# New TensorE durations in the planner of a two-block kernel: delta rounds and column norms

## The chip, the cores and the metric

The kernel runs on one core of one Trainium2 chip. The metric is the device time of one execution, in microseconds (us), from start to end on that core.

## The reference, cut to what matters

Two transformer-like blocks run one after the other on 1024 tokens of width 1024. The change touches the planning of two parts of the first block.

```python
# first block, delta branch: projection, depthwise convolution of 5 taps, silu, l2norm of q and k
qkv = silu(conv(concat([dq, dk, dv])))
dq, dk = dq * rsqrt(sum(dq * dq) + EPS), dk * rsqrt(sum(dk * dk) + EPS)   # per token and head of 128
# gated delta recursion, 4 heads of 128, two directions, chunks
def step(S, inp):
    v_new = u_c - w_c @ S
    o = (q_c * exp(g_c)) @ S + a_c @ v_new
    S = S * exp(g_last) + (k_c * exp(g_last - g_c)).T @ v_new
    return S, o
```

The same block has a neighbourhood attention branch; the second block has stick-breaking attention, chunked retention and three projections. The first block ends in an output projection whose input is the attention branch and the delta branch side by side, so the second block can't begin before the delta recursion is over.

## The kernel before, in words

**Layout.** All large projections are matmuls in three passes over split operands (`g` items: one of eight steps of one tile, lines 1781 to 1783 and 1787 to 1789). Weights come through a ring of raw buffers and are split into a high and a low part by ScalarE and VectorE (`w` items). The first block works through the blocks `dn0` to `dn3` (delta projections), `na0` to `na3` (attention), `dz` (gates), then has a stretch with no projection, in which the delta recursion is done, and then `wo0` and `wo1`, the output projection.

**The planner.** `schedule()` writes one list of items before anything is built. Class `Plan` keeps one clock for each engine, and streams (generators) that put items. `work(item)` gives an item's steps, each with an engine and a duration in ns. `put` moves each step to the later of the stream's time and its engine's clock, adds `HOP` (150 ns) after each step, and advances the engine's clock. `pump` lets every stream go on whose time is no later than TensorE's clock, in order of rank and time. Nothing of the durations is written into the kernel; what comes out is the order of the list. Every engine, and the DMA queues of SyncE and GpSimd, runs its part of the items strictly in the order of that list, with semaphore waits between engines. Which items exist, and what each does, doesn't depend on the durations. The order does, and with it the PSUM banks that `take` hands out to some of the items.

**The items that the change touches.**

- `cn` (h, c), eight of them, in the convolution's stream: 8 matmuls of 128x128 by one column, which sum the squares of the convolved q and k (line 1913), and a small evacuation on VectorE (line 2665).
- `r0` (h, s), the first third of round s of head h, for s from 1: 4 matmuls 128x128x128 (lines 1992 and 1995), then VectorE's residual (2725) and ScalarE's scaled copy of the query product beside it (2127 is the helper's line).
- `r1` (h, s): 2 matmuls (line 2011), then ScalarE's scaled copy and its plain copy of 128x256.
- `r2` (h, s): 2 matmuls for the state (line 2018, not in round 7) and 2 for the output (2023), then VectorE's update of the state (2735) and its add into the output (2742 and 2747).

**The items around them.** A round of a head is a chain: r0, r1, r2, and the next round's r0 waits for this round's state and output. Four heads, of 8 rounds each, run interleaved. A head may begin when its loads have landed (`dl`, `dv`, `dt` on SyncE's queue) and its levels `e0` to `e3` (a triangular inverse, lines 1950 to 1976) are done. After round 7 of a head come `f1` (square on ScalarE, line 2380; sums and a refined rsqrt on VectorE with ScalarE between, 2751 to 2759) and `f2` (two products of 128x1024 on VectorE, 2767 and 2770), then two `st mxd` items (transposes, line 1747). The other half of the output projection's input comes through `ld mix` (SyncE's queue), `mz` (GpSimd, 2972) and `st mix` (transposes). `wo0` begins when these are there.

Of the kernel before, what the change touches and what calls it, by code (L numbers as in the profile page):

```python
# [19 lines left out]
class Plan:  # L20
# [6 lines left out]
    def __init__(self, work):  # L27
        self.items, self.known = [], {}
        self.clock = dict(pe=0.0, act=0.0, dve=0.0, pool=0.0, dma=0.0, bus=0.0)
        self.streams, self.now, self.work = [], None, work  # L30
# [263 lines left out]
def work(item):  # L294
# [3 lines left out]
    def act(n):  # L298
        return "act", 170 + 0.87 * n

    def dve(n):
        return "dve", 130 + 1.08 * n
# [16 lines left out]
    if kind == "d9":  # L319
        return [("pool", 2700)]  # L320
    if kind == "r0":
        return [("pe", 450), ("dve", 690), ("act", 640, "beside")] if a[1] else []
    if kind == "r2":
        return [("pe", 450), ("dve", 620), ("act", 400) if a[1] == 0 else ("dve", 430)]
    if kind in ("ns", "np", "no"):
        n = 12 * COLS[a[2] % 4][1]
        return {"ns": [("pe", 60 if a[1] else 2.2 * n), dve(n + 90), act(n + 340)], "np": [("pe", 340), act(384)],
# [8 lines left out]
    if kind == "rm":  # L336
# [34 lines left out]
        "pa": [("dma", 4000)],  # L371
        "cs": [("act", 3700)],
        "cq": [act(1024)],
        "cn": [("pe", 900), ("dve", 150)],
        "d3": [("act", 900), ("dve", 400), ("act", 300)],
        "d4": [dve(1024)],
        "dm": [("pool", 1300)],
# [7 lines left out]
        "e1": [("pe", 800), ("dve", 850), ("act", 400, "beside")],  # L385
        "e2": [("pe", 500), act(512)],
        "e3": [("pe", 500), dve(512)],
        "r1": [("pe", 230), ("act", 640), ("act", 390)],
        "fz": [("dma", 5000)],
        "f1": [act(1024), dve(1024), ("dve", 300), ("act", 400), ("dve", 200)],  # L390
        "f2": [dve(1024), dve(1024)],
# [19 lines left out]
def schedule():  # L411

    plan = Plan(work)
    put, has = plan.put, plan.has
    place = {}
# [2755 lines left out]
```

How the kernel before makes its waits and increments, by code:

```python
    def wait_ge(self, sem, value):  # L123
        if self.seen.get(id(sem), 0) < value:
            self.seen[id(sem)] = value
            self.eng.wait_ge(sem, value)
# [1371 lines left out]
        def released(w, before):  # L1498
            if before:
                for said in freed(before):
                    w.wait_ge(*said)
# [64 lines left out]
        @block.sync  # L1567
# [3 lines left out]
            def load(n):  # L1571
                if n >= n_w:
                    return
                if n >= NRAW:
                    w.wait_ge(*at["w", n - NRAW, "lo"])
                if 72 <= n < 76:
                    for h in range(4):
                        w.wait_ge(*at["e3", h, 1, "o"])
                c0 = 0
                for s in weights(n)[1]:
                    wd = s.shape[1] if len(s.shape) == 2 else s.shape[1] * s.shape[2]
                    d = RAW[:, n % NRAW, c0:c0 + wd]
                    if len(s.shape) == 3:
                        d = d.rearrange("p (s c) -> p s c", c=s.shape[2])
                    e.dma_start(d, s).then_inc(c_raw[n % NRAW], 16)
                    c0 += wd
# [19 lines left out]
                    for n in range(72, 76):  # L1606
                        load(n)
                elif kind == "nx":
                    p = a[0]
                    w.wait_ge(*at["nz", p, "z"])
                    e.dma_start(z_d[p].rearrange("(t p) k -> p t k", p=128), tokens(p % 2)[:, :, 384:512]).then_inc(c_nz[p % 2], 16)
                elif kind == "gw":
                    w.wait_ge(*at["gr", "out"])
                    e.dma_start(g_d, GTs).then_inc(c_g, 16)
```

## Time and profile before

| what | value |
|---|---|
| median of 3 runs | 2236.14 us (2234.33 to 2240.19) |
| the profiled execution's own time | 2240.78 us |
| its span, first to last instruction | 2238.9 us |
| mean granted TensorE clock | 0.981 of full |
| TensorE matmuls busy | 2155.8 us (96%) |
| VectorE, ScalarE, GpSimd busy | 1086.3, 943.1, 386.1 us |

The profile is one execution with the hardware profiler. A busy TensorE is not TensorE at its peak, since matmuls overlap. The granted clock is a share of full speed, where 1.00 is 2.4 GHz and 0.50 is 1.2 GHz. Where a line says `x4`, four instructions of that line are merged; each 128x128 fp32 matmul of the source is two matmul instructions in the trace, a transpose is one.

### The profile page before, as it was taken

To read this page: it belongs to the slowest core of one execution; us is meant where nothing else is said; L and a number is where in the kernel's file an instruction comes from. 1 tells how busy PE (TensorE), PEld (TensorE's weight loads), DVE (VectorE), ACT (ScalarE), POOL (GpSimd) and SP (SyncE) were. 2 spreads that over 40 slices of the span, in tenths; PEclk is the share of its full clock that TensorE was granted. 3 is DMA by queue.
4 is the path that set the end of the run, shared out by engine and by line. 5 is a ranking of instruction groups with operands and counts; after the bars stand their busy time and mean duration, and the time that the engine had idled before them with its cause. 6 is when DMAs were issued, how large, how long until landed. Compare 5 with 4: busy or idle time off the path is not lost.

```text
span 2238.9 us, 29041 instructions
## 1 busy us (share of the span) xinstructions
PE 2155.8 (96%) x11559; PEld 1775.5 (79%) x11559; DVE 1086.3 (49%) x2025; ACT 943.1 (42%) x1712; POOL 386.1 (17%) x594
## 2 busy tenths in 40 slices
PE   7999999997887999999999999999999999999998
PEld 5787777776886888887888788887888878888887
DVE  5776444431366334667456755546425242433441
ACT  4655454553463234655455645643132313232220
POOL 5011452563013010000000000005202020110011
PEclk9999999999797999999999999999999999999999
DMA  4455454433724221122111111012221212344222
GB/s 146 134 191 180 115 147 127 109 98 119 310 70 165 72 86 38 39 71 62 48 34 57 57 57 39 29 33 71 85 71 34 62 34 88 101 157 140 94 93 86
DMA packets 169672, 209.76 MB, mean 94 GB/s; under 512 B 36320, under 2 KB 122816, under 8 KB 168000
## 3 DMA queue, kind: packets, MB, share of 16 engines
q1 hardware_dynamic: 148848, 140.71, 20.3%
q0 software_dynamic: 20688, 67.19, 9.4%
q8 instruction: 91, 1.49, 0.3%
q14 instruction: 45, 0.37, 0.1%
HBM read 150.41 MB, written 53.77 MB: 91 GB/s over the span
## 4 chain that ended last, share of the span: by engine, by line
PE 90%; DVE 3%; ACT 2%; DMA 2%; issue 2%; POOL 1%; SPq 1%; DVEq 0%; POOLq 0%; ACTq 0%
PE PS L1787 14%; PE PS L1789 13%; PE PS L1788 13%; PE PS L1781 9%; PE PS L1783 9%; PE PS L1782 9%; PE PS L1747 5%; PE PS L2073 3%; PE PS L2052 3%; PE PS L1882 2%; PE PS L2105 1%; PE PS L2118 1%; DMA WHF<-xe_d 1%; PE PS L1859 1%; DVE WH L2502 1%
## 5 line engine op out<-in xcount | busy, mean ns | idle before, releaser
L1787 PE MATMUL PS<-WH,HH 128*128 128x512 f32 x1344 | 549.5, 409 | 5.1 <-DVE WK L2557 5.1
L1789 PE MATMUL PS<-WH,HL 128*128 128x512 f32 x1344 | 527.3, 392 | 0.0
L1788 PE MATMUL PS<-WH,HH 128*128 128x512 f32 x1344 | 526.5, 392 | 0.0
L1781 PE MATMUL PS<-HH,WH 128*128 128x512 f32 (+1 forms) x976 | 399.1, 409 | 15.5 <-DVE WH L2502 12.1
L1783 PE MATMUL PS<-HH,WH 128*128 128x512 f32 (+1 forms) x976 | 383.1, 393 | 0.0
L1782 PE MATMUL PS<-HL,WH 128*128 128x512 f32 (+1 forms) x976 | 382.5, 392 | 0.0
L1787 PEld LDWEIGHTS PS<-WH,HH 128*128 128x128 f32 x1344 | 254.2, 189 | 61.4 <-issue 8.0
L1789 PEld LDWEIGHTS PS<-WH,HL 128*128 128x128 f32 x1344 | 253.8, 189 | 55.7
L1788 PEld LDWEIGHTS PS<-WH,HH 128*128 128x128 f32 x1344 | 254.9, 190 | 44.5
L2502 DVE SCALAR_TENSOR_TENSOR WH<-RAW,WK,WH 128x512 fp32r<-128x512 f32 (+2 forms) x248 | 183.5, 769 | 198.6 <-ACT WH L2127 198.2
L1781 PEld LDWEIGHTS PS<-HH,WH 128*128 128x128 f32 (+1 forms) x976 | 183.4, 188 | 54.2 <-DVE WH L2502 13.3
L2127 ACT ACTIVATE TM<-PS 128x512 f32<-128x512 f32 (+3 forms) x229 | 122.1, 545 | 238.4 <-PE PS L1789 148.7
L1783 PEld LDWEIGHTS PS<-HH,WH 128*128 128x128 f32 (+1 forms) x976 | 182.9, 187 | 41.4
L1782 PEld LDWEIGHTS PS<-HL,WH 128*128 128x128 f32 (+1 forms) x976 | 183.5, 188 | 35.9
L2127 ACT ACTIVATE WH<-RAW,WK 128x512 fp32r<-128x512 f32 (+2 forms) x248 | 167.3, 704 | 71.1 <-PE PS L1783 52.7
L2887 POOL DMA_DIRECT2D sig_d<-WK x32 | 17.6, 550 | 535.9 <-DVE WK L2573 535.9
L2555 DVE TENSOR_TENSOR WK<-TM 128x256 f32<-128x256 f32 x64 | 27.2, 425 | 167.6 <-ACT TM L2127 167.0
L1747 PE MATMUL PS<-WK,TM 128*128 128x128 f32 x584 | 87.8, 278 | 12.1 <-DVE TM L2836 6.2
L1747 PEld LDWEIGHTS PS<-WK,TM 128*128 128x128 f32 x584 | 71.8, 143 | 30.4 <-DVE TM L2836 7.2
L2127 ACT ACTIVATE WK<-PS,WK 128x512 f32<-128x512 f32 (+2 forms) x94 | 50.7, 565 | 100.6 <-PE PS L1747 98.5
L2814 DVE TENSOR_TENSOR_SCAN WK<-WK 128x639 f32<-128x639 f32 (+4 forms) x64 | 86.2, 1347 | 0.2
L2127 ACT ACTIVATE HH<-PS 128x512 fp32r<-128x512 f32 x64 | 35.5, 596 | 101.8 <-PE PS L1747 101.7
(316 smaller groups left out, 2895.5 us busy)
## 6 DMA issues: line engine op xcount, KB each, us to landing
RAW<-in_w_in SPq DMA_DIRECT2D x200, 256.0 KB, 3.2
RAW<-in_w_out SPq DMA_DIRECT2D x32, 256.0 KB, 3.6
sig_d<-WK POOLq DMA_DIRECT2D x32, 256.0 KB, 2.5
WK<-sig_d POOLq DMA_DIRECT2D x32, 256.0 KB, 3.2
WK<-in_rpb POOLq DMA_DIRECT2D x16, 480.0 KB, 4.7
RAW<-in_w_in SPq DMA_DIRECT2D x32, 192.0 KB, 5.3
dnc_d<-TM SPq DMA_DIRECT2D x12, 512.0 KB, 4.0
TM<-dnc_d SPq DMA_DIRECT2D x10, 512.0 KB, 4.8
```

The source lines that it names most:

```text
L1747: return e.transpose(o, i, ident[b:b + p, b:b + p] if p < 128 else ident)
L1781: e.matmul(ps, wh, hh, start=k == 0, stop=False)
L1782: e.matmul(ps, wh, hl, start=False, stop=False)
L1783: mm = e.matmul(ps, wl, hh, start=False, stop=k == 7)
L1787: e.matmul(ps, hh, wt[:, 0:width], start=k == 0, stop=False)
L1788: e.matmul(ps, hh, wt[:, 512:512 + width], start=False, stop=False)
L1789: mm = e.matmul(ps, hl, wt[:, 0:width], start=False, stop=k == 7)
L2052: mm = e.matmul(PS[:, z0 + c:z0 + c + n], chunk(L["q"], i), L["k"][:, c:c + n], start=True, stop=not last)
L2073: mm = e.matmul(bank(tb, 128), turned(h)[:, j, :], tokens(sb_buf(h))[:, j, 256:384], start=j == 0, stop=j == i)
L2127: return e.activation(o, i, ACT.Copy) if scale is None else e.activation(o, i, ACT.Copy, scale=scale)
L2502: stt(out=hl[:, 512:512 + width], in0=r, scalar=g, in1=hi, op0=ALU.mult, op1=ALU.subtract).then_inc(*w.sig(*item, "lo"))
L2814: e.tensor_tensor_scan(P, one.to_broadcast([128, (i + 1) * 128 - 1]), P, 0.0, ALU.mult, ALU.add).then_inc(*w.step())
```

## The change

Four entries of `work()` get other durations. The list of items, their instructions and their waits are what they were.

```diff
     if kind == "r0":
-        return [("pe", 450), ("dve", 690), ("act", 640, "beside")] if a[1] else []
+        return [("pe", 890), ("dve", 690), ("act", 720, "beside")] if a[1] else []
     if kind == "r2":
-        return [("pe", 450), ("dve", 620), ("act", 400) if a[1] == 0 else ("dve", 430)]
+        return [("pe", 890), ("dve", 660), ("act", 400) if a[1] == 0 else ("dve", 430)]
...
-        "cn": [("pe", 900), ("dve", 150)],
+        "cn": [("pe", 1750), ("dve", 150)],
...
-        "r1": [("pe", 230), ("act", 640), ("act", 390)],
+        "r1": [("pe", 440), ("act", 720), ("act", 390)],
```

## Rows read from the trace of the kernel before

**Rows 1.** The page: busy time of TensorE, and its granted clock in 40 slices.

```profile
PE 2155.8 (96%) x11559; PEld 1775.5 (79%) x11559; DVE 1086.3 (49%) x2025; ACT 943.1 (42%) x1712; POOL 386.1 (17%) x594
...
PEclk9999999999797999999999999999999999999999
```

**Rows 2.** Windows: stretch, its length, busy us of each engine (instructions), clock, DMA.

```profile
60.00:545.00 485.00, 465.71 (x2439) 375.24 (x2437) 248.79 (x596) 255.67 (x471) 161.35 (x287) 0.98 0.45 127
545.00:592.00 47.00, 31.31 (x515) 28.03 (x516) 10.00 (x20) 17.17 (x36) 7.58 (x5) 0.64 1.01 379
592.00:656.00 64.00, 61.01 (x871) 58.85 (x870) 38.28 (x108) 39.57 (x120) 5.81 (x8) 1.00 0.28 103
656.00:712.00 56.00, 35.39 (x234) 32.27 (x234) 41.48 (x87) 26.42 (x72) 20.92 (x21) 0.81 0.35 104
712.00:2239.00 1527.00, 1514.80 (x7296) 1246.38 (x7295) 714.98 (x1187) 578.03 (x984) 157.04 (x243) 1.00 0.22 71
```

**Rows 3.** Timeline of TensorE at 640 us: start, length, line, operation, how many.

```profile
639.84 0.61 PE L1992 MATMUL PS<-WHF,H 128*128 128x128 f32 x4
640.28 0.61 PE L1995 MATMUL PS<-WHF,H 128*128 128x128 f32 x4
640.73 0.61 PE L2018 MATMUL PS<-WHF,TM 128*128 128x128 f32 x4
```

**Rows 4.** Groups of instructions, 585 to 696 us: count, busy us, mean ns.

```profile
L2127 ACT ACTIVATE WHF<-PS,WK 128x128 f32<-128x128 f32 x96 | 29.2, 366 | 29.3 <-PE PS L1995 17.1 <-PE PS L2011 12.0
L2735 DVE SCALAR_TENSOR_TENSOR WHF<-WHF,WK,PS 128x128 f32<-128x128 f32 x36 | 10.8, 342 | 9.0 <-PE PS L2018 8.9
```

**Rows 5.** Timeline of 97 to 104 us, around the second column norm.

```profile
97.69 1.28 ACT L2298 ACT_TABLE_LOAD   x1
...
98.11 1.84 PE L1913 MATMUL PS<-WK,TM 128*128 128x1 f32 x16
...
101.36 1.12 ACT L2127 ACTIVATE WH<-RAW,WK 128x384 fp32r<-128x384 f32 x2
102.00 0.62 DVE L2502 SCALAR_TENSOR_TENSOR WH<-RAW,WK,WH 128x384 fp32r<-128x384 f32 x1 [3.68 <-ACT WH L2127]
102.54 1.28 DVE L2547 TENSOR_TENSOR TM<-PS,WHF 128x512 f32<-128x512 f32 x2
...
103.28 0.79 PE L1781 MATMUL PS<-HH,WH 128*128 128x512 f32 x1 [3.33 <-DVE TM L2547]
```

**Rows 6.** Timeline of TensorE: head 0's r0 of rounds 1 and 4, head 3's e0 and r1.

```profile
586.82 0.71 PE L1992 MATMUL PS<-WHF,H 128*128 128x128 f32 x4
...
614.34 0.61 PE L1992 MATMUL PS<-WHF,H 128*128 128x128 f32 x4
...
615.33 0.21 PE L1950 MATMUL PS<-RAW,WK 32*32 32x32 f32 x1
...
632.68 0.61 PE L2011 MATMUL PS<-TM,WK 128*128 128x128 f32 x4
```

**Rows 7.** Timeline of 668 to 675 us: head 1's f1 and what is behind it.

```profile
669.06 1.22 DVE L2751 TENSOR_REDUCE WK<-H 128x8 f32<-128x1024 f32 x1
...
671.28 0.60 DVE L2735 SCALAR_TENSOR_TENSOR WHF<-WHF,WK,PS 128x128 f32<-128x128 f32 x2
671.80 0.41 DVE L2747 TENSOR_TENSOR TM<-TM,PS 128x256 f32<-128x256 f32 x1
...
672.36 1.20 PE L1992 MATMUL PS<-WHF,TM 128*128 128x128 f32 x4 [3.72 <-DVE TM L2747]
```

**Rows 8.** Windows inside the tail of the recursion, columns as in rows 2.

```profile
672.30:678.00 5.70, 5.64 (x28) 5.63 (x28) 4.52 (x10) 2.10 (x6) 2.03 (x3) 0.55 0.01 3
```

**Rows 9.** Timeline of 693 to 712 us: the last head's end.

```profile
693.54 1.89 DVE L2767 TENSOR_TENSOR TM<-TM,WK 128x1024 f32<-128x1024 f32 x1
693.86 0.71 PE L2023 MATMUL PS<-WHF,WK 128*128 128x128 f32 x4 [0.47 <-ACT WHF L2127]
...
697.55 0.41 DVE L2747 TENSOR_TENSOR WK<-WK,PS 128x256 f32<-128x256 f32 x1
...
707.83 1.94 PE L1747 MATMUL PS<-WK 128*128 128x128 f32 x8 [6.40 <-DVE WK L2770]
```

## The prediction

> **What bounds the kernel now.** I read the page first, then windows of whole stages, then the timeline where windows show TensorE idle. The page says TensorE: it is busy 96% of the span [rows 1]. The change adds and removes no instruction, so TensorE's own work stays, and only what isn't work can move: idle time, and time at the lower clock. The windows say where that lies [rows 2]. From 712 us on, TensorE is idle 1527.0 - 1514.8 = 12.2 us, at clock 1.00. From 592 to 656, inside the recursion, it is idle 3.0 us of 64. From 656 to 712, the recursion's tail, it is idle 56.0 - 35.4 = 20.6 us, and the clock of 0.81 takes 0.19 x 56 = 10.6 us more (a little of it from idle time, where it costs nothing). From 60 to 545, the first block's projections with convolution and attention beside them, it is idle 19.3 us and the clock takes 0.02 x 485 = 9.7. From 545 to 592 it is idle 15.7 us with the DMA engines busy all the time (1.01): the loads of the recursion, which no order of compute shortens. So about 31 us can move in the tail and 29 us in the projections; nothing else that the changed items can reach is above noise.
>
> **The change, part by part.** First, are the new durations those of the trace? In the dense stretch, groups of four matmul instructions start at 639.84, 640.28 and 640.73: 0.445 us for four [rows 3]. r0 has 4 matmuls, 8 instructions, 0.89 us. r1 has 4 instructions, 0.445. r2 has 8, 0.89, but only 4 in round 7, where the new entry says double of what it costs. The column norm, 16 instructions, takes 1.84 us from first start to last end, about 1.7 us of the engine's time [rows 5], against the new 1750. ScalarE's scaled copies: two of 366 ns are 0.73 us; VectorE's state update: two of 342 ns are 0.68 [rows 4]. So the entries say what happens, with a small exception (four r2).
>
> **A rule beside it.** The Trainium skill, page "TensorE: Matmul & The Clock Gate", section "Back-to-back issue gap", gives about 81 ns as the sustained spacing of matmuls of 128 columns. By it r0 would be 8 x 81 = 650 ns (an estimate from that page) and the new entries would overstate TensorE by a third. The trace shows 111 ns for these fp32 instructions [rows 3], and I go by the trace.
>
> What the durations do is order. The planner's clock of TensorE gains 8 x 0.85 = 6.8 us in the convolutions, and 28 x 0.44 + 32 x 0.21 + 32 x 0.44 = 33.1 us in the recursion, if no planned idle time absorbs it. On the chip none of this is paid: cost in work, 0.
>
> **Column norms.** The first two stand where VectorE and ScalarE are late. The row that matters is the wait at 103.28: the next block's first tile waits 3.33 us for an evacuation on VectorE, which sits behind a weight split, which waited 3.68 us for ScalarE, which had two silu passes with their table loads ahead of it [rows 5]. That is the largest stall of the stage. I worked the planner's list through over the first norm. The norm's end moves by 0.85, one silu (the third part of head 0) comes one or two places earlier, before a weight split and not after it, and the evacuation that the tile waits for still comes behind the same two weight splits. Both silus are still ahead. So this stall stays, to within the one weight split of 0.6 us. From there on the whole list is shifted by up to 6.8 us against the streams whose times come from DMA or ScalarE, and waits of 1 to 2 us form and vanish at other places. I can't give the sign. Bounds: all of the stage's 29 us gained is not reachable, since most of its waits hang on attention chains that the norms don't touch. I take 0, with -4 to +4 (a seventh of what can move, each way).
>
> **The rounds, while TensorE is full.** A head's round in the planner is the sum of its steps and hops. Before: 450 + 690 + 230 + 640 + 390 + 450 + 620 + 430 + 8 x 150 = 5.10 us. After: 890 + 690 + 440 + 720 + 390 + 890 + 660 + 430 + 1200 = 6.31. So each planned round gets 1.2 us longer, while the moment at which the next head's loads are thought to land stays. What moves: the levels (e0 to e3) of heads 2 and 3 come earlier in the list, measured in rounds of heads 0 and 1. Size, from the trace: head 0 goes from round 1 to round 4 between 586.82 and 614.34, 9.2 us a round; head 3's e0 follows at 615.33 [rows 6]. Three rounds of head 0 lose 3.6 planned us, 0.4 of a round; head 1, with two rounds, loses 0.3. A round is 2.23 us of TensorE (0.89 + 0.445 + 0.89). So 0.7 x 2.23 = 1.6 us of work of heads 0 and 1 slides behind head 3's levels, and head 3 (first r1 now at 632.68, the last to finish) starts up to 1.6 us earlier. Is its data there? The window's DMA share falls from 1.01 before 592 to 0.28 after, so by 613 it is. The dense stretch itself gains nothing: what slides comes back in the same full stretch.
>
> **The tail.** Here two heads are left and the chains decide. Two waits are of the order's making. Head 1's f1 (sum, refinement, with ScalarE between) stands on VectorE from 669.06, ahead of head 2's state update, which begins at 671.28; TensorE waits 3.72 us [rows 7], and the clock after it is 0.55 over 5.7 us, which takes 2.6 more [rows 8]. And head 2's f2 products, from 693.54, stand ahead of head 3's last add: its matmuls end at 694.57, the add starts at 697.55, 3.0 us later, and head 3's own f1, f2 and transposes follow, 6.40 us of idle TensorE [rows 9]. The new order has such blocks too: f1 and f2 of a head are put when its round 7 is planned done, whatever the durations, and four of them must go between or behind the rounds. Truer durations make it likelier that what is put ahead is what is ready first, which speaks for a small gain; head 3's earlier start speaks for at most 1.6 us. Against: if heads end closer together, more f1 and f2 work is left for the end, where nothing covers it (VectorE is busy 41.5 of 56 us there already [rows 2]). I take -2 us, bounds -9 (both waits gone: 3.7 + 2.6 + 3.0) and +7.
>
> **Sum.** 0 (work) + 0 (projections, -4 to +4) - 2 (recursion) = -2 us. Against the profiled execution's own 2240.8 us that is 2238.8. That execution is 4.6 us above the median of the runs shown (2236.1), so on the median's scale it is 2234.
>
> On clock: after the 3.72 us wait the granted clock falls to a mix of 1.2 and 2.4 GHz [rows 8]. The Trainium skill, same page, section "HAM oscillation — how this bites in real kernels", counts half of the throttled time as lost; the row agrees, and I use the row.
>
> **The rivals.**
>
> *A. The tail's order improves for good.* Both waits above vanish, and nothing takes their place: -9.3 us, with some luck in the projections -11: 2225 to 2227. For it: both waits come from a position on VectorE, and durations were wrong by half exactly there. Against: f1 and f2 keep their own durations and their own trigger.
>
> *B. A new block on the last head (the slower side).* One f1 with its f2 is put ahead of a round of head 3 while no other head has work for TensorE. Place: VectorE, after head 2's round 7. Price: sum 1.2 and refinement 1.0 (671.28 - 669.06 less the sum) [rows 7], two products 4.0 (697.55 - 693.54) [rows 9], so 6.2 us on the last chain, and one more low clock of 2.6 [rows 8]: 8.8 us. Less the 2 us that I expect otherwise, that is +7, 2243. It decides when head 3 is more than one round behind head 2 in the plan but ready in fact; the overstated r2 of round 7 (0.45 us too long) and longer planned rounds both push that way. A shift in the projections by its +4 bound alone doesn't reach it.
>
> *C. The order hardly changes.* Rounds are put by a rule that mostly goes round the four heads, and the list could come out nearly the same: 0, 2236.
>
> *D. The constants overshoot.* If planned idle time doesn't absorb the 33 us, the planner thinks that TensorE is the late engine and lets the streams run far behind; items of loads and transposes for `wo0` (mix) are then put later among the rounds. The last mix transpose costs 1.1 us after the last head's, so this is worth at most +2: 2238.
>
> **How the numbers follow.** No change of this kernel below 0.3%, 6.7 us, can be told from none. Forecast (a shift between -6 and +6 with -2 as its middle, C and D in it): 0.62. A and other gains past 6.7 us: 0.22. B and other losses past it: 0.16. The range is to leave out no more than 0.2: the forecast alone is 2229 to 2241; to it I add most of A and most of B, which gives 2226 to 2243.
>
> **What would show it right or wrong.** Right: matmul counts equal; 712 us and after unchanged in length; the 3.3 us wait near 103 us still there; head 3's first r1 some 1 to 3 us earlier relative to head 0's first; idle TensorE from the last loads to `wo0` within 3 us of 23.6. Wrong: the wait at 103 us gone or doubled, with the stage's length changed by more than 4 us; the tail longer or shorter by more than 5 us; or the second block's stalls moved, which I hold fixed because its order is planned from full TensorE work in both.

## The result, and the profile after

The changed kernel takes 2263.88 us (median of 4 runs, 2260.9 to 2264.77), the kernel before 2236.91 beside it (2234.33 to 2240.19). The ratio is 1.0117, interval 1.0104 to 1.013: **27 us slower**, where 2234 (2226 to 2243) was predicted. The profiled execution took 2264.77 us, its span is 2263.0, against 2240.78 and 2238.9 before.

The page of the changed kernel, its lines for busy time and granted clock:

```profile
PE 2167.5 (96%) x11559; PEld 1787.4 (79%) x11559; DVE 1086.3 (48%) x2025; ACT 943.0 (42%) x1712; POOL 386.8 (17%) x594
...
PEclk9999989989597999999999999999999999999999
```

The instruction counts are those of [rows 1], and so are the busy times of VectorE and ScalarE. TensorE's count is the same and its busy time 12 us more, and the granted clock has new dips at 283 to 340 and 453 to 509 us, and a deeper one (5 instead of 7) at 566 to 622. Windows of the changed kernel, with the stretches of [rows 2] (only the last one ends later, as the span does):

```profile
60.00:545.00 485.00, 455.07 (x2368) 367.63 (x2367) 249.47 (x595) 252.61 (x467) 153.39 (x270) 0.95 0.42 124
545.00:592.00 47.00, 32.15 (x324) 26.91 (x323) 5.82 (x10) 11.39 (x17) 17.77 (x22) 0.71 0.78 270
592.00:656.00 64.00, 61.42 (x966) 58.38 (x965) 28.50 (x75) 34.78 (x100) 2.18 (x3) 0.84 0.52 202
656.00:712.00 56.00, 43.52 (x354) 41.85 (x354) 39.82 (x108) 31.03 (x95) 14.85 (x17) 0.96 0.27 81
712.00:2262.00 1550.00, 1527.58 (x7348) 1257.97 (x7347) 729.50 (x1209) 586.52 (x1001) 165.16 (x251) 0.99 0.22 71
```

In 60 to 545 us TensorE gets through 2368 matmul instructions where it got through 2439. Its idle time is 485 - 455.1 = 29.9 us and not 19.3, and the clock is 0.95 and not 0.98. The other windows hold shifted work and can't be compared by the clock on the wall. Landmarks can. In the table the last two columns are in us, counted from the span's start to the landmark: TensorE's idle time, and half of its busy time at 1.2 GHz ("half-clock"), which is what that clock cost.

| landmark | before | after | shift | idle / half-clock before | after |
|---|---|---|---|---|---|
| first product of `na2` | 323.5 | 321.7 | -1.8 | | |
| `na2`, fifth tile | 357.4 | 369.6 | +12.2 | | |
| `na3` | 404.6 | 409.7 | +5.1 | | |
| gate projection `dz` | 476.0 | 497.2 | +21.2 | 31.1 / 10.1 | 42.2 / 15.9 |
| first transpose of the recursion's loads | 551.2 | 567.2 | +16.0 | 38.0 / 10.1 | 48.6 / 17.2 |
| head 0's first r1 | 578.9 | 594.7 | +15.8 | | |
| head 3's first r1 | 632.7 | 647.8 | +15.1 | | |
| `wo0` | 711.6 | 734.1 | +22.5 | | |
| end | 2232.4 | 2256.3 | +23.9 | | |

So 16 us are lost in the projections with attention beside them, before the recursion begins, 7 in the recursion's tail, and 1 in the second block. (`dz` starts 21 us late, but with the last pair's attention already done; 5 us come back by the first transpose.) The 3 us to the 27 lie between executions: the profiled one of before was 3.9 us above the median of its four, that of the changed kernel 0.9. Both losses are traced below to the order of the list.

**First loss, 332 to 347 us.** GpSimd's instructions over 300 to 345 us. Of before:

```profile
323.98 8.09 POOL L2887 DMA_DIRECT2D mix_d<-TM  x16 [13.15 <-DVE TM L2624]
332.06 9.02 POOL L2887 DMA_DIRECT2D WK<-TM  x16
```

Of the changed kernel:

```profile
320.07 9.11 POOL L2887 DMA_DIRECT2D WK<-TM  x16 [7.48 <-PE PS L1882]
329.17 8.08 POOL L2887 DMA_DIRECT2D mix_d<-TM  x16
```

The line with `mix_d<-TM` is `nw(0)`, the write of the first attention pair's result to `mix_d`; the one with `WK<-TM` is the four gathers `nv(1, *)` of the next pair, 2.3 us each. They have changed places. In the changed kernel the write stands behind 9.1 us of gathers, and is issued 5.2 us later than before (with a rule that puts it ahead of the gathers, it goes at 320.90, in experiment 4). Who waits for that can be seen in the timeline of 333 to 342 us of the changed kernel:

```profile
339.62 0.69 ACT L2127 ACTIVATE TM<-PS,WK 128x512 f32<-128x512 f32 x1 [4.73 <-DMA mix_d<-TM]
...
340.34 0.43 DVE L2555 TENSOR_TENSOR PS<-TM 128x256 f32<-128x256 f32 x1 [9.11 <-ACT TM L2127]
...
341.28 0.80 PE L1787 MATMUL PS<-WH,HH 128*128 128x512 f32 x1 [6.84 <-DVE WK L2557]
```

Read upwards: TensorE waits 6.84 us for VectorE, VectorE 9.11 for ScalarE, ScalarE 4.73 for the transfer. The evacuation of `na2`'s first tile goes into the buffer from which `nw(0)` still reads. The window of 335 to 347 us, first of before, then of the changed kernel:

```profile
335.00:347.00 12.00, 12.00 (x63) 9.47 (x62) 6.21 (x21) 5.20 (x13) 6.09 (x11) 1.00 0.97 238
```

```profile
335.00:347.00 12.00, 5.72 (x15) 4.51 (x16) 3.25 (x12) 2.60 (x6) 2.25 (x5) 0.57 0.55 100
```

TensorE was full there, and is now idle for 6.3 us and at clock 0.57.

**Second loss, 485 to 500 us.** The same two kinds of item for pairs 2 and 3. GpSimd at 455 to 510 us, of before, then of the changed kernel:

```profile
469.77 8.13 POOL L2887 DMA_DIRECT2D mix_d<-TM  x16 [0.35 <-POOL TM L3005]
478.46 9.01 POOL L2887 DMA_DIRECT2D WK<-TM  x16 [0.56 <-ACT TM L2127]
```

```profile
483.30 9.08 POOL L2887 DMA_DIRECT2D WK<-TM  x16 [0.37 <-PE PS L1859]
494.27 8.10 POOL L2887 DMA_DIRECT2D mix_d<-TM  x16 [0.58 <-POOL TM L3005]
```

`nw(2)` may be put only after `d9(1, 14)`, the last of 15 parts of the second inversion (GpSimd's 3005). That now comes behind the gathers of the last pair. `dz` is put only when the item after that inversion (`da(1)`) is there, so the last pair's attention stands alone ahead of `dz`, with nothing to cover its chains. The cost is not in GpSimd's queue here, as it is in the first loss: TensorE's waits are for ScalarE, and it is the planner's condition on `da(1)` that sets `dz` behind them. TensorE of the changed kernel:

```profile
485.31 0.86 PE L1747 MATMUL PS<-WK 128*96 128x128 f32 x6 [2.05 <-ACT WK L2255]
491.48 1.08 PE L1747 MATMUL PS<-WK,TM 128*128 128x128 f32 x4 [5.30 <-ACT WK L2127]
492.49 1.65 PE L1859 MATMUL PS<-WK 64*128 64x384 f32 x4
494.07 2.82 PE L1882 MATMUL PS<-WK 96*128 96x64 f32 x12
```

At these times of before TensorE was full of `dz` products: the window 475 to 545 has 69.3 us busy at clock 1.00 before, 62.7 at 0.90 after.

The swap is not all that is late there. The whole second inversion is, by 13 us, while `na3` is by 5. Its first instruction, before and in the changed kernel:

```profile
431.85 0.26 POOL L3002 TENSOR_TENSOR WK<-TM 128x30 f32<-128x30 f32 x1
```

```profile
444.81 0.25 POOL L3002 TENSOR_TENSOR WK<-TM 128x30 f32<-128x30 f32 x1
```

### The profile page after: what moved, and what is told of

Its sections match the earlier page's. It is cut to its first block, busy times and chain, and to the rows that moved or that the text cites. A ratio compares the mean times of both kernels' runs of the same rounds, so it can differ in the third digit from the quotient of the medians.

```text
span 2263.0 us, 29060 instructions
## 1 busy us (share of the span) xinstructions
PE 2167.5 (96%) x11559; PEld 1787.4 (79%) x11559; DVE 1086.3 (48%) x2025; ACT 943.0 (42%) x1712; POOL 386.8 (17%) x594
## 4 chain that ended last, share of the span: by engine, by line
PE 89%; DVE 4%; ACT 2%; DMA 2%; POOL 1%; issue 1%; SPq 1%; DVEq 0%; POOLq 0%; ACTq 0%
PE PS L1787 13%; PE PS L1789 13%; PE PS L1788 13%; PE PS L1781 9%; PE PS L1783 9%; PE PS L1782 9%; PE PS L1747 5%; PE PS L2073 3%; PE PS L2052 3%; PE PS L1882 2%; DVE WH L2502 1%; PE PS L2105 1%; PE PS L2118 1%; DMA WHF<-xe_d 1%; PE PS L1859 1%
## 5 line engine op out<-in xcount | busy, mean ns | idle before, releaser
L1789 PE MATMUL PS<-WH,HL 128*128 128x512 f32 x1344 | 528.0, 393 | 0.0
L1747 PE MATMUL PS<-WK,TM 128*128 128x128 f32 x584 | 89.4, 281 | 17.5 <-ACT WK L2127 9.9
L2073 PEld LDWEIGHTS PS<-TM 128*128 128x128 f32 x576 | 73.0, 191 | 6.6 <-issue 2.2
```

The lines of the kernel that those rows point to most:

```text
L1747: return e.transpose(o, i, ident[b:b + p, b:b + p] if p < 128 else ident)
L1789: mm = e.matmul(ps, hl, wt[:, 0:width], start=False, stop=k == 7)
L2073: mm = e.matmul(bank(tb, 128), turned(h)[:, j, :], tokens(sb_buf(h))[:, j, 256:384], start=j == 0, stop=j == i)
```

## The experiments

Theory T: the loss before the recursion is two swaps in GpSimd's queue, made by the column norms' entry alone, each a threshold. Rivals: the loss is in proportion to the norms' duration (a later and later list); or it comes from the rounds' entries; or the swaps are only signs of a general lateness. Edits are shown against the kernel before, except the first of 4, which adds its rule to the changed kernel. Several were timed together with the kernel before, whose medians beside them were 2236.92, 2237.78, 2238.25 and 2239.2 us; so ratios are compared, not medians. A hundredth of a per cent of the ratio is 0.22 us.

**1. The halves: only the norms' entry, only the rounds' entries.**

```diff
-        "cn": [("pe", 900), ("dve", 150)],
+        "cn": [("pe", 1750), ("dve", 150)],
```

> Only the column norm's duration is changed (900 to 1750); the rounds' durations are those of before. Theory 1 (the norm's duration flips the order in the attention stage): the recursion's first transpose is 14 to 18 us late, the recursion keeps its length, and the median is 2251 to 2256. Rival (the loss needs both changes, through the recursion's start): less than 5 us, under 2242.

Measured: 2255.24 us (2253.04 to 2260.27), ratio 1.0081 (1.0056 to 1.0106).

```diff
-        return [("pe", 450), ("dve", 690), ("act", 640, "beside")] if a[1] else []
+        return [("pe", 890), ("dve", 690), ("act", 720, "beside")] if a[1] else []
...   (r1 and r2 as in the change, cn left at 900)
```

> Only the rounds' durations are changed; the column norm keeps 900. Everything up to the recursion is ordered as before. Theory 1: the projections are unchanged and the recursion is 5 to 8 us longer (as it is in the changed kernel, 6.5 us from its first transpose to the output projection), median 2241 to 2245. Rival (the recursion's longer stretch came from its late start and the clock it found): 0 +- 3 us, 2234 to 2240.

Measured: 2240.96 us (2231.1 to 2246.07, 10 runs), ratio 1.001 (0.9993 to 1.0026). So the norms alone give 18 us of the 27, with both swaps in the trace (`nv(1, *)` at 320.10, `nw(0)` at 329.19) and `dz` at 497.1, as in the changed kernel. The rounds alone give 2 by the ratio (its interval is -2 to +6) and can't be told from none; the time lies between the two ranges that were expected. The two don't add up to 27; see 6.

**2. Is it in proportion? The norms' entry at 1500 and at 1100.**

```diff
-        "cn": [("pe", 900), ("dve", 150)],
+        "cn": [("pe", 1500), ("dve", 150)],
```

> Only the column norm's duration is changed, to 1500, that is by 0.7 of the change. Theory 1 (a flip of the order at a threshold): the list keeps the mix write of head pair 0 ahead of the next pair's gathers on GpSimd's queue, and the time is that of before within 4 us, 2233 to 2241. Rival (the loss grows with the duration, because the planner's TensorE clock runs further ahead of the other engines): 0.7 of the loss, +11 us, 2248.

Measured: 2235.08 us (2229.33 to 2237.32, 10 runs), ratio 0.9987 (0.9973 to 1.0).

```diff
-        "cn": [("pe", 900), ("dve", 150)],
+        "cn": [("pe", 1100), ("dve", 150)],
```

> Only the column norm's duration is changed, to 1100, by 0.24 of the change. Theory 1 (a flip, here again on the bad side: the four gathers stand ahead of the mix write, and the second inversion's last part behind the last pair's gathers): nearly the whole loss, +12 to +18 us, 2249 to 2255. Rival (the loss grows with the duration): +4 us, 2241.

Measured: 2258.59 us (2256.32 to 2263.18), ratio 1.0096 (1.007 to 1.0121). A quarter of the change costs as much as the whole (the intervals overlap), and 70% of it costs nothing. That is no proportion. The 22 us are more than was expected, too. At 1500 the write stands first in both places (320.23, gathers 328.30), `dz` starts at 471.4; at 1100 the gathers do (323.78, write 332.86), `dz` starts at 500.2.

It is not one threshold for each swap either. `schedule()`, run with 22 entries from 900 to 1950 in steps of 50 (the planner alone, not the chip), has both swaps at 1100, 1150 and 1550 to 1750, and neither at any other entry: they come and go together, after an earlier choice in the list. The traces show that something earlier differs. The first inversion's last instruction on GpSimd starts at 301.05 us before and at 295.98 with 1500, but at 311.41 with 1100 and 308.34 with 1750. Which item turns there was not traced, and no entry above 1750 was run.

**3. Each swap by itself, in the kernel before, with its old durations.** In `na_back`, ahead of `put("nw", p)`:

```diff
+            if p == 0:
+                yield lambda: ("nv", 1, 3) in plan.known
```

> The kernel before, with one rule more: the mix write of head pair 0 is put behind the four gathers of pair 1, as it stands in the changed kernel; the second inversion keeps its place. If the write's place is a cause by itself: TensorE waits 6 to 7 us once, near 335 to 345 us, behind an evacuation that waits for the write, with a low clock after it (some 4 us more), and the median rises by 5 to 11 us, 2242 to 2248. Rival (the write's place only goes along with the late inversion, which is the whole cause): within 3 us of before. The planner itself sees 1.3 us in this.

Measured: 2245.92 us (2245.32 to 2247.22), ratio 1.0039 (1.0026 to 1.0052). The wait is there. Timeline of this kernel, 336 to 350 us, and its window:

```profile
340.04 0.69 ACT L2129 ACTIVATE TM<-PS,WK 128x512 f32<-128x512 f32 x1 [7.94 <-issue]
340.76 0.43 DVE L2557 TENSOR_TENSOR PS<-TM 128x256 f32<-128x256 f32 x1 [10.81 <-ACT TM L2129]
...
343.79 0.90 PE L1749 MATMUL PS<-WK 128*128 128x128 f32 x3 [5.17 <-DVE TM L2626]
```

```profile
338.00:352.00 14.00, 8.84 (x36) 6.78 (x35) 6.02 (x22) 5.34 (x13) 0.91 (x3) 0.76 0.23 65
```

ScalarE's 7.94 us have no releaser in this profile ("issue"). That they are for the write's transfer, as the 4.73 us in the changed kernel, is concluded from the same instruction at the same place: the write's issues end here at 338.60, there at 337.25.

In `invert`, ahead of `put("d9", n, part)`:

```diff
+            if (n, part) == (1, 14):
+                yield lambda: ("nv", 3, 3) in plan.known
```

> The kernel before, with one rule more: the last part of the second inversion is put behind the four gathers of pair 3, as it stands in the changed kernel. If the inversion's place is a cause by itself: the gate projection starts 9 to 14 us later, with TensorE idle or on attention work alone before it, and the median rises by 6 to 13 us, 2243 to 2250. Rival (only the write's place costs): within 3 us of before.

Measured: 2246.66 us (2243.09 to 2250.75), ratio 1.0042 (1.0027 to 1.0058), with the wait of the changed kernel in TensorE's timeline and `dz` at 490.4:

```profile
485.25 1.09 PE L1749 MATMUL PS<-WK,TM 128*128 128x128 f32 x4 [4.66 <-ACT WK L2129]
```

Each swap alone costs 8 to 9 us (8.1 and 8.9 by the medians, each with an interval 6 to 7 us wide), together 17 to 18, and the norms' entry alone cost 18. That they add up so well is partly luck, since the rest of the list follows each of them differently. In the kernel with the second swap alone the inversion begins at 431.50, as before, so the 9 us are the price of its last part's place and not of a late inversion.

**4. Take the swaps out of the changed kernel.** In `na_gather(p)`, after its wait for `no(p - 1, 1, 7)`:

```diff
+            yield lambda: ("nw", p - 1) in plan.known
```

For p = 3 this also brings `d9(1, 14)` ahead of the gathers, since `nw(2)` waits for it. First with all the new durations, then with the norms' alone:

> The changed kernel, with one rule more: the gathers of a head pair are put only after the mix write of the pair before. The 6.8 us wait near 341 us is gone, and with it, by the planner's order, the last inversion part comes ahead of the last pair's gathers too. Of the projections' 16 us some 10 to 14 come back; the recursion stays as in the changed kernel. Median 2249 to 2254. Rival (the loss is in the shift of the solve stream, which this doesn't undo): 2260 to 2264.

Measured: 2247.27 us (2241.41 to 2250.47), ratio 1.0042 (1.0026 to 1.0058).

> The true column norm and the rule of the write before the gathers, with the rounds' durations of before: the partner of the changed kernel with that rule (2247.3), from which it differs in the rounds alone. If the rounds' order costs 2 to 3 us everywhere and the rest of the 8.7 us was the clock: 2243 to 2246. Rival (the rounds cost 8 us whenever the norm is 1750): 2237 to 2241.

Measured: 2242.8 us (2240.55 to 2249.09, 10 runs), ratio 1.0022 (1.001 to 1.0033). The rule takes the changed kernel from 27 us above before to 9.5 above, more than was expected, and the norms' half from 18 to about 5 (3.6 by the medians). `dz` starts at 478.6 and 480.6 us (476.0 before). GpSimd of the first of them has the order of before:

```profile
320.90 8.09 POOL L2888 DMA_DIRECT2D mix_d<-TM  x16 [8.44 <-DVE TM L2625]
328.98 9.04 POOL L2888 DMA_DIRECT2D WK<-TM  x16
```

TensorE in it still waits 3.72 us for VectorE at 337.57, where before had none. So the rest is no swap of these two, and what it is in the list was not taken apart.

The rule undoes more than the swaps. The second inversion begins at 433.48 and 435.51 us, not at 444.81, so these two runs don't take the second swap out by itself. The first inversion stays late (its last instruction starts at 308.19 and 310.20, 301.05 before). So the rival of a general lateness is out for the whole loss, since that lateness without the swaps costs some 5 us (2 to 7 by the interval), and it stands for those 5.

**5. A version that beats both.** By the planner's own clock (not the chip's) the list of before was a good draw. I varied the two fixed delays of the convolution's stream over 30 settings for either duration of the norms, without the rule of 4. The planned end of the last `dz` product, with the norms' true cost of 6.8 us added to it under the old entry, had a median of 534.2 us with the old entry (523.5 to 555.1; this kernel's own 529.3) and of 528.0 with the new one (522.0 to 541.4; the change's own 541.4, the worst of its 30). The best, together with the rule of 4:

```diff
-        "cn": [("pe", 900), ("dve", 150)],
+        "cn": [("pe", 1750), ("dve", 150)],
...   (na_gather as in 4)
-        plan.now[0] += 2500.0
+        plan.now[0] += 1500.0
...
-            plan.now[0] += 6000.0
+            plan.now[0] += 6500.0
```

> The true column norm (1750), the rule of the write before the gathers, and the two margins in the convolution's stream changed (6000 to 6500 ns before the norm, 2500 to 1500 before the store), the rounds' durations of before. By the planner's own clock, less the 6.8 us that a true norm adds to it, the recursion's loads come 7 us earlier than in the kernel before. If the planner's clock can be used to choose: median 2227 to 2233. Rival (the planner's clock tells flips but not a few us): 2234 to 2240.

Measured: **2230.3 us** (2225.21 to 2233.53, 7 runs), ratio 0.9963 (0.9949 to 0.9977): 8 us faster than before. The rule has no part in it: without it `schedule()` gives the same list at these delays. What the run shows is one better list, found by the planner's clock. Its page:

```profile
PE 2149.3 (97%) x11559; PEld 1770.5 (80%) x11559; DVE 1086.3 (49%) x2025; ACT 942.5 (42%) x1712; POOL 384.1 (17%) x594
...
PEclk9999999998898999999999999999999999999999
```

`dz` starts at 466.3 us, 9.7 earlier than before, with 27.8 us idle and 3.1 of half-clock loss up to it (31.1 and 10.1 before). The same with the rounds' new entries too:

> The kernel of the previous experiment (true norm, write before gathers, the two margins) with the changed kernel's durations of the rounds too. It differs from that one in the rounds alone. If the true rounds cost in every context (as in the two pairs so far: +2 to +4 us and +8.7 us): 2233 to 2240. Rival (the 8.7 us came from the clock that the changed kernel's recursion happened to find): the same as the previous one within 2 us, 2228 to 2232.

Measured: 2232.22 us (2228.21 to 2237.31, 10 runs), ratio 0.9972 (0.9957 to 0.9988).

**6. What the rounds do.** TensorE's durations of the rounds alone, and the other engines' (720 and 660) alone:

```diff
-        return [("pe", 450), ("dve", 620), ("act", 400) if a[1] == 0 else ("dve", 430)]
+        return [("pe", 890), ("dve", 620), ("act", 400) if a[1] == 0 else ("dve", 430)]
...   (r0 and r1 in the same way)
```

> The kernel before with only the TensorE durations of the rounds changed (890, 440, 890), not those of ScalarE and VectorE. If the longer TensorE steps bring head 3 forward and leave more f1 and f2 work at the end: head 3's first product comes 3 to 5 us earlier after head 0's, and the tail from there to the output projection is 5 to 7 us longer; median 2238 to 2243. Rival: the evictions' durations do it, and this is within 2 us of before.

Measured: 2236.39 us (2232.21 to 2243.32, 10 runs), ratio 0.9993 (0.9979 to 1.0006). The expected order came (head 3 3.9 us earlier, tail 4.5 longer, table below), the expected time didn't.

```diff
-        return [("pe", 450), ("dve", 620), ("act", 400) if a[1] == 0 else ("dve", 430)]
+        return [("pe", 450), ("dve", 660), ("act", 400) if a[1] == 0 else ("dve", 430)]
...   (r0 and r1 in the same way)
```

> The kernel before with only the rounds' evictions changed (720, 720, 660). If the TensorE durations carry the effect: within 2 us of before, 2235 to 2239. Rival: 2239 to 2243.

Measured: 2240.62 us (2234.79 to 2243.86, 10 runs), ratio 1.0005 (0.9992 to 1.0017). Neither can be told from none. The changed kernel once more, to learn whether its recursion is always as in the first trace:

> The changed kernel once more, beside the previous one on one chip. If the long stretch at the lower clock at the start of the recursion belongs to this order: the low clock ends again about 45 us after the recursion's first transpose, and the median is 2261 to 2265. Rival (it is a state that any of these kernels finds in some executions): it ends at 31 to 35 us, and the times come down to 2255 to 2260.

Measured: 2260.71 us (2258.35 to 2264.51), ratio 1.0101 (1.0083 to 1.0119). The stretch at the lower clock ends 31.4 us after the first transpose, as the rival said, and the median lies between the two ranges. The recursion in the profiled executions, each stretch in us from landmark to landmark (head 0's first r1, head 3's first r1, `wo0`):

| rounds' entries | kernel | to head 3 | to `wo0` | sum |
|---|---|---|---|---|
| old | before | 53.8 | 78.9 | 132.7 |
| old | norms at 1750 | 54.3 | 78.9 | 133.2 |
| old | norms and rule | 53.7 | 78.9 | 132.6 |
| old | version of 5 | 53.9 | 78.9 | 132.8 |
| new | rounds only | 49.0 | 86.1 | 135.1 |
| new | after, with rule | 48.4 | 86.3 | 134.7 |
| new | version of 5 | 47.1 | 86.6 | 133.7 |
| new | after, second profile | 48.8 | 86.6 | 135.4 |
| new | after, first profile | 53.1 | 86.4 | 139.5 |
| TensorE's new | the first kernel of 6 | 49.9 | 83.4 | 133.2 |
| other engines' new | the second kernel of 6 | 56.0 | 82.1 | 138.1 |

Four more executions with old entries have sums of 131.4 and 131.6 (norms at 1500 and 1100), 131.7 and 136.6 (the second and the first swap alone). 138.1 and 136.6 belong to executions with a long stretch at the lower clock, as 139.5 does. Each of the four kernels with all new entries has its counterpart with old ones. The new rounds bring head 3 forward by 4.8 to 6.8 us and pay 7.2 to 7.7 in the tail: 0.9 to 2.4 us worse in the four rows above the first profile's, the same sign each time. The ratios of the timed pairs give 2 (rounds only), 2 (5 with and without) and 4.5 (after with rule against norms with rule; the second timing of after against the norms alone). The 53.1 of the first profile is something else, told in the last section.

## Why the prediction was wrong

**The step that failed** is the term of the projections: "I take 0, with -4 to +4 (a seventh of what can move, each way)". It measured +16 in the traces and +18 in time. That it is the norms' entry and no other is shown (1), and that it doesn't go by the size of the entry is shown (2). That the two changed places carry most of it is shown by making each alone (3), 8 to 9 us each; that some 13 of the norms' 18 us, and 18 of the 27, go with them when they are undone is shown too (4), though there the second inversion moves as well. The bound was a share of what can move, which fits many small shifts. Here nothing was shared out: a pair of items on an in-order queue either stands one way or the other, and one way costs 8 us. Two parts of that step were false. "most of its waits hang on attention chains that the norms don't touch": the norms' entry moved those very chains, because the write and the gathers of the attention are ordered against a clock that the norms set. And the 29 us that could move were those lost already; time that was full [rows 2, and the window of 335 to 347 above] can be lost as well, and was.

**What could have been read beforehand.** The trace of before shows the write at 323.98 and the gathers right behind it, with no idle time between, on a queue of which the text ahead says that it runs strictly in order, and TensorE full at 335 to 347. A tie between two items of 8 and 9 us, one of which has a waiting reader, is the thing to price. The Trainium skill, page "TensorE: Matmul & The Clock Gate", section "Architectural detail: the array is 16× 32×32, not 1× 128×128", calls GpSimd strictly first in, first out for each of its cores; the trace agrees, the write goes at 329.17 when the gathers' 9.11 us from 320.07 are over. And the prediction followed the planner's list by hand for the first norm only. The planner's own clock, run with both durations, puts `dz` 24.5 us later, of which 6.8 are the longer entries themselves and 17.7 the order; the chip had it 21.2 later. It is no sure guide either: for the first swap alone it showed 1.3 us where the chip took 8.

**The wait near 103 us stays**: right in size, its order nearly. The changed kernel at 99 to 104 us:

```profile
100.94 0.62 DVE L2502 SCALAR_TENSOR_TENSOR WH<-RAW,WK,WH 128x384 fp32r<-128x384 f32 x1 [7.77 <-ACT WH L2127]
101.48 1.28 DVE L2547 TENSOR_TENSOR TM<-PS,WHF 128x512 f32<-128x512 f32 x2
...
102.21 0.79 PE L1781 MATMUL PS<-HH,WH 128*128 128x512 f32 x1 [2.69 <-DVE TM L2547]
```

It is 2.69 us and was 3.33 [rows 5]: "to within the one weight split of 0.6 us". But the evacuation doesn't come "behind the same two weight splits": 20 splits of line 2502 stand ahead of it in the trace, and 21 did before. This care went to a stall that was there, and none to those that weren't yet.

**The entries say what the chip does**: right [rows 3, 4], and of no help. Truer durations made this list worse, though by the planner's clock they make the middle one of 30 lists better (5).

**Head 3 earlier by up to 1.6 us**: right in sign, 5 measured (53.8 to 48.8 or 49.0; in the first profile only 0.7, with the lower clock for 14 us longer). The 0.7 of a round that was reckoned came out as about two rounds of 2.23 us.

**The tail, "I take -2 us, bounds -9 and +7"**: the sign was wrong, the bound held. Counted from head 3's first r1 the tail grows by 7.5 us, where the head start gives 5: net +1 to +4.5 instead of -2. The reason named as "against", heads ending closer together, is not what the traces show. With the rounds' entries alone the last r2 of heads 2 and 3 start at 681.1 and 698.6 us, 17.5 apart; before it was 686.0 and 693.9. One of the two waits priced for the tail is even gone: the last add of head 3 starts 0.4 us after its matmuls end (699.66, 700.08), where it was 3.0. But head 3 takes 73.3 us from its first r1 to its last r2, and took 61.2; so it ends 4.7 us later, though it began 7.4 earlier, and `wo0` starts at 711.5 us, before at 711.6. In all five traces with the rounds' new entries it takes 72.8 to 73.8 us. Part of it is seen on TensorE's queue in that kernel: a transpose of the other half of the output projection's input, which waits for GpSimd (line 2972), and head 2's transposes (eight instructions at 695.19) now stand ahead of head 3's last r1 and r2; before, head 2's stood behind them (697.78, the last r2 at 693.86).

```profile
694.31 1.09 PE L1747 MATMUL PS<-WK,WHF 128*128 128x128 f32 x4 [2.74 <-POOL WHF L2972]
```

No run swaps this place alone, so its price isn't known. In the changed kernel TensorE's last wait before `wo0` is 7.37 us, for the same f2 product of the last head as the 6.40 in [rows 9]:

```profile
730.77 1.94 PE L1747 MATMUL PS<-WK 128*128 128x128 f32 x8 [7.37 <-DVE WK L2770]
```

**The rivals.** A (both waits of the tail gone, 2226) was in no run; with the new rounds one of them went, for no gain. B had the sign and the kind of mechanism, something put ahead on an in-order engine with low clock behind it, and priced one at 8.8 us; the swaps cost 8.1 and 8.9, a match of size by luck, since their terms are others. But it looked for the place on VectorE at the end of the recursion. The places were in the attention stage, with GpSimd's items out of turn, and there were two of them. "A shift in the projections by its +4 bound alone doesn't reach it" took the failed bound as given. C's time held for the rounds, within what can be measured, though the order did change. D's mix items did come among the last rounds: the wait of 2.74 us above is for one of them. The second block was held fixed, and it moved by about 1 us.

**What stays open.** Which item of the list turns first, and brings both swaps, is not known. Why the rule leaves 5 us (norms) and not 0 was not taken apart; the planner's clock has 4.5 us of it (`dz` 11.3 later, 6.8 of them the longer entries). Nor was it settled why the two halves, 18 and 2, make 24 to 27 together; 4.5 rather than 2 us for the rounds is within what the intervals allow.

## What to carry to other kernels

A duration in a planner acts only through the order that it makes, so its effect comes in jumps, and not even in one direction: 200 ns more cost 21 us here, 600 ns more nothing, 850 ns more 18. Before such a change, list the pairs of items that sit back to back on an in-order queue, and the items that may be put only after another (as `dz` after `da(1)`), ask of each what waits if they swap, and make the costly ones explicit rules; correct durations don't protect them. And judge a duration not by one list but by a family of lists with small other delays changed, since the kernel that is there may be a lucky draw, whose luck any change ends.

## What the runs showed of the hardware

The stretch at 1.2 GHz that begins with the loads of the recursion (in three traces with a break of 3.4 us) ends 31 to 35 us after the first transpose in twelve of the profiled executions, and 43 to 46 us after it in three. Two executions of the same kernel, the changed one, differ in it. Windows at the same place, first profile, then second:

```profile
590.00:600.00 10.00, 7.58 (x179) 7.15 (x180) 1.91 (x5) 4.34 (x11) 0.00 (x0) 0.50 1.01 387
600.00:610.00 10.00, 10.00 (x79) 9.32 (x79) 2.19 (x5) 2.19 (x5) 0.00 (x0) 0.50 1.02 411
```

```profile
590.00:600.00 10.00, 9.45 (x197) 8.76 (x193) 2.10 (x5) 4.94 (x13) 0.00 (x0) 0.54 1.01 382
600.00:610.00 10.00, 9.62 (x141) 8.93 (x141) 5.06 (x12) 5.18 (x15) 0.00 (x0) 1.00 1.03 413
```

In the first TensorE is 10.00 us of 10 busy at clock 0.50 and gets 79 matmul instructions done, in the second 141. In the 10 us ahead of that it was busy 7.58 against 9.45. Over 50 us from the first transpose half of the busy time at 1.2 GHz is 18.1 us in the first and 12.7 in the second. These 5.4 us belong to no order; 4.1 of them can be seen between the two profiles' rows in the table of 6. A single profile would have put them down to the change.
